# A streaming encoder step on one core: layer-norm sums gathered during the products, and the last weight chunk run one output tile at a time

## The reference, cut to what matters

```
def layer_norm(x, g, b):
    mu  = mean(x, -1)
    var = mean(square(x - mu), -1)
    return (x - mu) * rsqrt(var + 1e-5) * g + b

x = layer_norm(alpha * x + mixer(x),           ln_g[l,0], ln_b[l,0])   # ln00, ln10
x = layer_norm(alpha * x + cross_attention(x), ln_g[l,1], ln_b[l,1])   # ln01, ln11
x = layer_norm(alpha * x + mlp(x),             ln_g[l,2], ln_b[l,2])   # ln02, ln12
```

## Time and profile before

| What | us or share |
|---|---|
| median of three executions | 3120.66 |
| profiled execution, its own time | 3126.84 |
| profiled execution, span from first to last instruction | 3125.0 |
| TensorE (PE) busy with matmuls | 3039.7 (97%) |
| VectorE (DVE) busy | 1888.6 (60%) |
| ScalarE (ACT) busy | 412.6 (13%) |
| GpSimd (POOL) busy | 91.6 (3%) |
| share of the chain that ended last: PE, DVE | 89%, 7% |
| mean granted TensorE clock, 1 being 2.4 GHz | 0.986 |

### The profile page before, as it was taken

How to read it: one execution, slowest core, us unless ns; L and a number is a source line. 1 busy time by engine, 2 the same in 40 slices (tenths; PEclk the granted TensorE clock), 3 DMA queues, 4 the chain that set the end, 5 groups by cost and what they waited for, 6 DMA issues and landing times.

```text
span 3125.0 us, 47497 instructions
## 1 busy us (share of the span) xinstructions
PE 3039.7 (97%) x20530; PEld 2862.8 (92%) x20530; DVE 1888.6 (60%) x1485; ACT 412.6 (13%) x763; POOL 91.6 (3%) x64
## 2 busy tenths in 40 slices
PE   7999999899999999999999997999999999999999
PEld 6888899689989899999999996898999999999997
DVE  5666666546735765555665567744676555656565
ACT  2000003310220211000110003311031100011001
POOL 0000000100000000000000001000000000000000
PEclk9999999889999999999999998999999999999999
DMA  6666754234444355555555551453445555555552
GB/s 224 218 217 216 222 179 125 86 108 148 136 147 131 118 168 161 163 168 166 161 161 164 169 163 62 156 165 108 148 135 165 169 163 161 161 166 170 162 161 84
DMA packets 432690, 489.02 MB, mean 156 GB/s; under 512 B 16801, under 2 KB 388279, under 8 KB 431223
## 3 DMA queue, kind: packets, MB, share of 16 engines
q1 hardware_dynamic: 421344, 453.01, 46.3%
q0 software_dynamic: 4432, 18.15, 1.7%
q10 hardware_dynamic: 6836, 16.73, 1.4%
HBM read 476.47 MB, written 11.40 MB: 156 GB/s over the span
## 4 chain that ended last, share of the span: by engine, by line
PE 89%; DVE 7%; ACT 1%; DMA 1%; issue 1%; DVEq 0%; ACTq 0%
PE ps L217 24%; PE ps L219 23%; PE ps L218 23%; PE ps L370 4%; PE ps L371 4%; PE ps L372 4%; DVE WL L1334 3%; DVE X L1573 1%; PE ps L433 1%; PE ps L713 1%; PE ps L689 1%; DVE XL L1568 1%; DVE WH L1332 1%; PE ps L585 1%; PE ps L680 0%
## 5 line engine op out<-in xcount | busy, mean ns | idle before, releaser
L217 PE MATMUL ps<-XH,WH 128*128 128x288 f32 x3760 | 1118.3, 297 | 27.8 <-DVE XL L1339 11.8
L219 PE MATMUL ps<-XH,WL 128*128 128x288 f32 x3760 | 1111.2, 296 | 0.0
L218 PE MATMUL ps<-XL,WH 128*128 128x288 f32 x3760 | 1110.3, 295 | 0.0
L1334 DVE TENSOR_TENSOR WL<-RAW,WH 128x2048 fp32r<-128x2048 f32 x433 | 1019.0, 2353 | 14.8
L217 PEld LDWEIGHTS ps<-XH,WH 128*128 128x128 f32 x3760 | 708.2, 188 | 37.3 <-issue 17.1
L219 PEld LDWEIGHTS ps<-XH,WL 128*128 128x128 f32 x3760 | 708.1, 188 | 0.0
L218 PEld LDWEIGHTS ps<-XL,WH 128*128 128x128 f32 x3760 | 707.8, 188 | 0.2
L1332 DVE CAST WH<-RAW 128x2048 fp32r<-128x2048 f32 x433 | 528.4, 1220 | 220.3 <-DMA RAW<-in_xa_wk 58.5
L217 PE MATMUL ps<-HH,WH 128*128 128x288 f32 x2048 | 606.5, 296 | 1.7 <-DVE WL L1334 1.7
L219 PE MATMUL ps<-HH,WL 128*128 128x288 f32 x2048 | 603.9, 295 | 0.0
L218 PE MATMUL ps<-HL,WH 128*128 128x288 f32 x2048 | 603.1, 295 | 0.0
(11 more groups left out here) (252 smaller groups left out, 1634.9 us busy)
## 6 DMA issues: line engine op xcount, KB each, us to landing
RAW<-in_mlp_up SPq DMA_DIRECT2D x128, 1024.0 KB, 5.4
RAW<-in_mlp_down SPq DMA_DIRECT2D x128, 1024.0 KB, 5.3
RAW<-in_xa_wk SPq DMA_DIRECT2D x32, 1024.0 KB, 5.7
RAW<-in_xa_wv SPq DMA_DIRECT2D x32, 1024.0 KB, 5.3
RAW<-in_xa_wq SPq DMA_DIRECT2D x32, 1024.0 KB, 5.3
RAW<-in_xa_wo SPq DMA_DIRECT2D x32, 1024.0 KB, 5.3
RAW<-in_w_in SPq DMA_DIRECT2D x22, 1024.0 KB, 5.4
RAW<-in_w_out SPq DMA_DIRECT2D x16, 1024.0 KB, 5.3
```

Of the source, the lines that this page charges most:

```text
L217: nc.tensor.matmul(out, wh, xh, start=start, stop=False)
L218: nc.tensor.matmul(out, wh, xl, start=False, stop=False)
L219: return nc.tensor.matmul(out, wl, xh, start=False, stop=stop)
L1334: V.tensor_tensor(WL[:, s, 0:n], RAW[:, s, 0:n], WH[:, s, 0:n].bitcast(f32), ALU.subtract).then_inc(chunk_split, 1)
```

## The change

Five layer-norms (all but ln10) get their sums while the products still run.

- After the first body of `wout`, `wo` and `downb` (4 of the 16 tiles of X), VectorE adds up those four tiles, TensorE sums them with ones (`shift_sum`), and ScalarE copies the result times 4 into SHIFT: the mean of the first quarter of the features. VectorE subtracts it from all four quarters of X (`shift`), those not yet reached being scaled by alpha at once; later outputs are added to the shifted X without a scale.
- ScalarE squares each quarter when it is complete. VectorE adds up X into YSUM and the squares into the first tile of SQ, quarter by quarter. GpSimd's `add_up` is gone.
- The last chunk runs all 8 input tiles for output tile 14, then all for 15. Between the two TensorE sums the folded 14 tiles of both kinds. Tiles 14 and 15 are added, squared and summed by themselves, and the variance is the mean of squares less the square of the mean.
- Split chunks run one chunk further ahead from the third body on. The hardware loops over these bodies are written out.
- After the sums X is processed in groups of 1, 1, 2, 4, 4 and 4 tiles: VectorE subtracts the mean and multiplies by 1/std, ScalarE applies gain and offset to each tile and copies the group to XH, VectorE writes XL for the group. ln10 keeps its own sums, and uses the same groups.

The diff, cut:

```diff
-        def chunk_mms(h, bank, rhs, first, final):
+        def chunk_mms(h, bank, rhs, first, final, ln=None):
...
+            for m in range(2):
+                for k in range(8):
...
+                if m == 0:
+                    mm.then_inc(sem(f"{ln}_stat"), 1)
+                    pe.wait_ge(*reached(f"{ln}_folded", 2))
+                    one_sum(4, YSUM[:, 0, :], True, False)
+                    one_sum(5, SQ_OF[ln][:, 0, :], True, False)
...
+                    if shift and j == 0:
+                        shift_sum(shift)
...
+        def shift_sum(ln):
+            pe.wait_ge(*reached(f"{ln}_folded", 1))
+            one_sum(4, SQ_OF[ln][:, 14, :], True, True).then_inc(sem(f"{ln}_stat"), 1)
+
+        def statistics(name, ln, bridge=4):
+            pe.wait_ge(*reached(f"{name}_out1", 4))
+            one_sum(4, X[:, 14, :], False, False)
+            pe.wait_ge(*reached(f"{ln}_sq", 5))
+            one_sum(5, SQ_OF[ln][:, 14, :], False, False)
+            pe.wait_ge(*reached(f"{name}_out1", 5))
+            one_sum(4, X[:, 15, :], False, True).then_inc(sem(f"{ln}_stat"), 1)
+            pe.wait_ge(*reached(f"{ln}_sq", 6))
+            one_sum(5, SQ_OF[ln][:, 15, :], False, True).then_inc(sem(f"{ln}_stat"), 1)
+            keep_clock(bridge)
...
+                    if shift and j == 1:
+                        shift_sum(shift)
...
-            variance(f"ln{l}2", bridge=(12, 4)[l])
+            keep_clock((12, 4)[l])
...
+        def affine(ln, l, s):
+            for n, (k0, k1) in enumerate(GROUPS):
+                act.wait_ge(*reached(f"{ln}_v", n + 1))
+                for k in range(k0, k1):
+                    A(X[:, k, :], X[:, k, :], ACT.Identity, scale=LNG(l, s, k), bias=LNB(l, s, k)
+                      ).then_inc(sem(f"{ln}_x"), 1)
+                act.wait_ge(*reached(f"{ln}_x", k1))
+                A(XH[:, k0:k1, :], X[:, k0:k1, :], ACT.Copy).then_inc(sem(f"{ln}_high"), 1)
...
-        def add_up(name):
...
+        def shifted_phase(name, per, alpha, ln, first_split=False, before=None):
...
+            chain(grow(sq[:, 12:14, :], X[:, 0:2, :], X[:, 2:4, :]))
+            grow(sq[:, 14, :], sq[:, 12, :], sq[:, 13, :]).then_inc(sem(f"{ln}_folded"), 1)
+
+            for j in range(per):
+                next_split(1, j)
+                if j == 0:
+                    dve.wait_ge(*reached(f"{ln}_coef", 1))
+                    shift(1)
+                    dve.wait_ge(*reached(f"{ln}_s", 1))
+                if j % half == half - 1:
+                    add(1, j // half)
+                if j == half - 1:
+                    shift(0)
+                if j == half:
+                    shift(2)
+                if j == per - 1:
+                    shift(3)
...
+            for j in range(per):
+                next_split(3, j)
...
+                if j == half:
...
+                    V.tensor_tensor(YSUM[:, 0:2, :], YSUM[:, 0:2, :], X[:, 12:14, :], ALU.add)
+                    dve.wait_ge(*reached(f"{ln}_sq", 4))
+                    chain(grow(sq[:, 0:2, :], sq[:, 0:2, :], sq[:, 12:14, :]))
+                    grow(YSUM[:, 0:2, :], YSUM[:, 0:2, :], YSUM[:, 2:4, :])
+                    chain(grow(sq[:, 0:2, :], sq[:, 0:2, :], sq[:, 2:4, :]))
+                    grow(YSUM[:, 0, :], YSUM[:, 0, :], YSUM[:, 1, :])
+                    grow(sq[:, 0, :], sq[:, 0, :], sq[:, 1, :]).then_inc(sem(f"{ln}_folded"), 1)
+            dve.wait_ge(*reached(f"{ln}_stat", 2))
+            V.tensor_tensor(X[:, 14, :], X[:, 14, :], ps[:, 2, 0:T], ALU.add).then_inc(sem(f"{name}_out1"), 1)
+            dve.wait_ge(chunk_used, c0 + 4 * per)
+            V.tensor_tensor(X[:, 15, :], X[:, 15, :], ps[:, 3, 0:T], ALU.add).then_inc(sem(f"{name}_out1"), 1)
...
+        def ln_to_split(ln):
+            spread(ln, GROUPS[0], GROUPS[1])
+            scaled(ln, 0, *GROUPS[0])
+            scaled(ln, 1, *GROUPS[1])
+            centre(ln, 2, *GROUPS[2])
+            scaled(ln, 2, *GROUPS[2])
+            low(ln, 0)
+            low(ln, 1)
+            for n in (3, 4, 5):
+                centre(ln, n, *GROUPS[n])
+                scaled(ln, n, *GROUPS[n])
+                low(ln, n - 1)
+            low(ln, 5)
```

More of the change, by code:

```diff
@@ L133, in build @@
     OST = area("OST", [P, 3, 320], 69248)
-    SQ = area("SQ", [P, NK, T], 0)
+    SQA = area("SQA", [P, NK, T], 0)
+    SQX = sb("SQX", [P, NK, T], lay["XL"])
+    SQ_OF = {"ln00": SQA, "ln01": SQA, "ln02": SQX, "ln10": SQA, "ln11": SQA, "ln12": SQX}
     QX = area("QX", [P, NK, T], 0)
@@ L191, in reached @@
             names, per = KINDS[KIND_OF[which]]
-            before = sum(per[what] for w in names[:names.index(which)] if (w, what) not in NOT_SIGNALLED)
+            count = per[what] if isinstance(per[what], dict) else {w: per[what] for w in names}
+            before = sum(count.get(w, 0) for w in names[:names.index(which)])
         return sem(name), n + before
     SAMPLE_UNIT = 3
+    GROUPS = [(0, 1), (1, 2), (2, 4), (4, 8), (8, 12), (12, 16)]
+    group_from = {k0: n for n, (k0, _) in enumerate(GROUPS)}
     PHASES, c = {}, 0
@@ L648, in _ @@
         pe.wait_ge(sem("mla_ol"), NU)
[L649 to L652, removed]
+        for i in range(4):
+            linear_body("wout", i, shift="ln00" if i == 1 else None, last="ln00" if i == 3 else None)
+        statistics("wout", "ln00")
         def cross_attention(l):
@@ L752, in cross_attention @@
                         if k in (0, 12) else None)
[L753 to L756, removed]
+            for i in range(1, 4):
+                linear_body(f"wo{l}", i, shift=f"ln{l}1" if i == 1 else None, last=f"ln{l}1" if i == 3 else None)
+            statistics(f"wo{l}", f"ln{l}1")
         def mlp(l):
@@ L769, in mlp @@
                 else:
-                    residual_sums(f"{dn}{l}")
+                    for i in range(4):
+                        down_body(f"{dn}{l}", f"{up}{l}", i, shift=f"ln{l}2" if i == 1 else None,
+                                  last=f"ln{l}2" if i == 3 else None)
+            statistics(f"downb{l}", f"ln{l}2", bridge=0)
             if l == 0:
@@ L1312, in _ @@
         memory(1)
-        add_up("wo1")
-        add_up("downb1")
     @block.vector
@@ new lines, in inverse_root, with spread @@
+        def inverse_root(ln):
+            dve.wait_ge(*reached(f"{ln}_coef", 1 if ln == "ln10" else 3))
+            chain(V.reciprocal(RS[:, :], RS[:, :]))
+        def spread(ln, first, second):
+            dve.wait_ge(*reached(f"{ln}_coef", 2))
+            dve.wait_ge(*reached(f"{ln}_stat", 4))
+            V.tensor_tensor(RS[:, :], ps[:, 5, 0:T], MEAN2, ALU.subtract).then_inc(sem(f"{ln}_folded"), 1)
+            centre(ln, 0, *first)
+            centre(ln, 1, *second)
+            inverse_root(ln)
```

371 lines of the change are left out of this document (222 added, 149 removed).

## The result

The changed kernel takes 3100.53 us (median of 14 runs, 3091.46 to 3114.02), the kernel before in the same comparison 3118.74 (14 runs, 3109.61 to 3126.32): a ratio of 0.9945, 95% interval 0.9933 to 0.9957, so 13 to 21 us less. The forecast was 3102, 18.5 less.

What follows compares the result with a forecast made beforehand. TensorE carries 89% of the chain of waits, so time is won only where it stops. Tails 16.8 + ln02 3.5 - ln12 1.2 - ln10 0.6 = 18.5 off 3120.66: 3102 us, range 3088 to 3115.

Steps and rivals of the forecast that it cites:

- The waits in downb: downb0 and downb1, second body: VectorE's split queued behind its wait for SHIFT stops TensorE 5.7 us; -7.2 per phase.
- Rival 1: Wait in downb is covered, VectorE being further ahead or SHIFT earlier: 14.4 us return, 3088; chance 0.12.
- The tails: After ln00, ln01, ln11: last product to third chunk 26.2 instead of 33.14 us, gain 6.9; net 5.6 each, 16.8 together.
- Rival 3: Layer-norm's end isn't early: 1 us more per handover of the five last groups, 3116, no difference; chance 0.06.
- Costs against the tails: Per tail: three added sums 1.5 us, stall at the folded sums 0.4; against these, GpSimd's additions going gives +1.2.
- Rival 2: Folds come late in wout and wo too: each of three phases loses 3.5 us, 3112; chance 0.12.
- The clock: Behind the tails' new gaps TensorE runs partly at 1.2 GHz: 0.6 us per tail, between 0 and 3.
- Rival 4: TensorE stays at 1.2 GHz behind its new gaps: 24.3 + 7.2 = 31.5 us lost, 3133.5, slower; chance 0.05.
- ln02: Layer-norm before the pooling: gain between 8 and 12.7 us, taken as 11; net 3.5 with sums, POOL's additions and downb wait.
- the rule named beside the forecast: Pooling: GpSimd shuts out only VectorE instructions with two SBUF inputs, so centring never waits; gain 12.7, total 1.7 larger.
- ln12: Bare tail at the kernel's end: ScalarE ends at 16.6 instead of 22.86 us, 6.3 gained; net -1.2 after costs.
- Written-out loops and the order of the last chunk: Bodies' loops and last chunk's 48 reordered matmuls: both priced at nothing; loops bounded at 0 to 3 us.

Runs made afterwards that it cites:

- the first two experiments: Changed kernel, second down phases: TensorE's sum for SHIFT one chunk earlier, 3086.42 us (0.9891); or VectorE's next split ahead of its wait for SHIFT, 3085.93 us (0.9885).

## Why the prediction was right, step by step

- **The waits in downb**, forecast -7.2 each: the stretches became 7.32 and 7.48 longer, with the new sums and the gain from GpSimd in them. The mechanism (VectorE's split behind the wait for SHIFT) is shown by the first two experiments, its price by the first: 7.25 and 7.39 come back. The idle time was 5.57 for 5.7, and 13 matmuls in 3.00 us at half speed (1.73 at the full rate) are 1.3 for the 1.5 I took. Rival 1, the covered wait, is out.
- **The tails**, forecast 6.9 shorter to the third chunk: 6.22. The term that was off is ScalarE's affine: 0.43 taken from an operation with an offset alone, 0.52 measured with gain and offset. Without the gain the tail is 0.65 shorter, which is nearly the whole difference. The Trainium skill ("ScalarE: Activation LUTs", "What ACT_TABLE_LOAD costs") prices each such per-partition operand at some 93 ns, and the trace agrees (2.19 less 1.81, a quarter of it: 0.095); I should have added it. ln10 has the same groups with its old sums and lost by them, which speaks for the early sums, not the groups, as what the tails won by; no run has the one without the other in these three, so that division is argued and not shown.
- **Rival 3**, a price at each handover, is out at its size: it would have made each tail some 5 us longer than 26.2, and they last 27.05. The first product of upa0 comes 8.22 after the last of wo0, where I had 8.45 after the sums.
- **Costs against the tails.** wo0 came out 0.15 longer. GpSimd's additions gave back 1.37 when removed alone, for 1.2; so the three sums take about 1.5, as forecast, and nothing is left for a stall of the folds. (I had put 0.4 for it; 2 x 6.37 + 6.37 + 3.18 is 22.3 and not 22.2, so my own terms gave 0.2.) TensorE has no idle time in the products of wo0 and wo1. Rival 2 is out.
- **The clock** behind the new gaps, 0.6 forecast for each tail: in ln01 the first group ran at half speed (granted clock 0.54), in ln00 it did not (1.00), and both tails last 27.05. Cover made it free. Rival 4, 8.7 for each tail and 3.6 more behind each downb wait, is out by its size.
- **ln02**, forecast 11: 11.88. The first window came at 12.5 after the last product, for 11.1 after the sums; the second `windows` at 25.8, for 28.2 at the best. The centring never waits for POOL, so the rule named beside the forecast was the better price for that step than the bound I chose between. That the gain still came out at 11.88 is in part luck: I took the start of the second `windows` for the whole, and of the 15.3 by which it came earlier 2.6 went into that operation itself (4.08 for 1.47, beside the last addition on POOL) and 0.8 behind it. The stage also varies: 77.2 to 79.3 in three profiles of kernels with the old layer-norm, 65.2 to 65.7 in six profiles of variants with the change's code in it.
- **ln12**, forecast 6.3 before its costs: X is finished 17.4 after the last product instead of 23.0, which is 5.6. Of the missing 0.7 the last four affines make 0.43 (2.18 for 1.75). To the end of the span it is 5.99, but what follows X varies: the stage takes 27.9 here and 28.3 to 29.1 in other profiles with the same code in it. **ln10**, forecast -0.6: -1.67. Here ScalarE is the supply; dropping the gain gives 1.17 back.
- **Written-out loops and the order of the last chunk**, forecast at nothing: shown by experiment for TensorE's loops and for the order, each within 0.1 us in an output projection with its tail. VectorE's loops were written out too; no run has that alone.

The sum by measured terms is 18.2 for three tails with their phases (forecast 16.8), 4.6 for ln02 with downb0 (3.5), -1.5 for ln12 with downb1 (-1.2), -1.7 for ln10 (-0.6): 19.6, where 18.5 stood. That it lies within 1.1 is closer than its terms are: 2.5 too little in the first two stands against 1.4 too much in the others, and in each tail the clock (0.6) and the stall (0.4), which weren't there, made up for the affine (0.7).

## What to carry to other kernels

When an engine in the middle of a pipeline gets a new wait, look at what stands behind it in its queue, not at how idle it is: here VectorE idled 8 us and its next split, needed by TensorE, was behind the wait. Put the producer's step a chunk earlier, or the urgent work ahead of the wait; either won back 14 us of a change that had won 18. In a tail bound by supply, shortening the last group pays only until the group before it, and the consumer's own work behind it, is last; and slack before the consumer also hides a slow clock, so removing the slack can bring its cost out (1.3 us in one of three tails here).

## What the runs showed of the hardware

TensorE's half-speed stretches move: stages with the same code have them on different work in different kernels' profiles (granted clock 0.65 and 0.57 at different places of cross-attention, 0.70 and 0.91 in the same 20 us of the first attention). The stages differ with it, by 1.7 us in each cross-attention and some 6 us in the first attention. In the tails they cost nothing where TensorE waits anyway and 1.3 us where it doesn't. The comparison of the two single profiles at the top carries 8 us from stages without an edit, nearly half of what the change did; the stages have to be compared one by one.
